# Compressed-key layers: VectorE's floors and inverses three steps ahead and behind the minima, the window keys' copies ahead of the second floor

## What is computed

```python
out = lax.map(block, (qb_all, gates, jnp.arange(n_q)))
...
s_s = jnp.einsum('btgrd,bgtnld->bgrtnl', qb, kg).astype(f32) * scale
s_s = s_s - slopes[None, :, :, None, None, None] * dist_s[:, :, None]
p_s = masked_softmax(s_s, (dist_s >= 0)[:, :, None], (-2, -1))
o_sel = jnp.einsum('bgrtnl,bgtnld->btgrd', p_s.astype(vg.dtype), vg)
...
p_w = masked_softmax(s_w, mask_w, -1)
o_win = jnp.einsum('bgrtl,blgd->btgrd', p_w.astype(vw.dtype), vw)
return gb[..., 0:1] * o_cmp + gb[..., 1:2] * o_sel + gb[..., 2:3] * o_win
...
def masked_softmax(s, mask, axis):
    s = jnp.where(mask, s, NEG_INF)
    m = jnp.max(s, axis=axis, keepdims=True)
    e = jnp.where(mask, jnp.exp(s - m), 0.0)
    return e / jnp.maximum(jnp.sum(e, axis=axis, keepdims=True), 1e-30)
```

## Time and profile before

| | before |
|---|---|
| median of 3 runs | 2573.88 us (2573.37 to 2575.04) |
| time of the profiled execution | 2574.38 us |
| its span | 2572.6 us |
| mean granted TensorE clock | 0.996 |
| busy: TensorE, VectorE, ScalarE, GpSimd | 98%, 62%, 46%, 18% |

### The profile page before, as it was taken

The page is one execution under the profiler, slowest core; times in us unless marked ns, Lnnn a source line. Parts: engine busy times, 40 slices in busy tenths (PEclk is TensorE's granted clock), DMA queues, the critical chain, the costliest instruction groups (busy, mean ns, idle before and its releaser), DMA issues.

```text
span 2572.6 us, 38307 instructions
## 1 busy us (share of the span) xinstructions
PE 2514.6 (98%) x13336; PEld 2072.8 (81%) x13336; DVE 1607.4 (62%) x2773; ACT 1184.5 (46%) x2035; POOL 467.3 (18%) x514
## 2 busy tenths in 40 slices
PE   8999999999999999999999999999999999999997
PEld 6987778888788678888878878888779778788886
DVE  7598577664353847667256677664386884766733
ACT  4467554443232845444245554443254684544431
POOL 2035321110010612111010021110010552111100
PEclk9999999999999999999999999999999999999999
DMA  4410123333233023332321123333233002233331
GB/s 160 142 34 2 42 83 98 98 98 98 87 99 99 9 66 99 98 97 90 103 85 57 42 82 99 98 98 98 79 116 122 18 2 58 87 94 97 90 106 49
DMA packets 61909, 210.91 MB, mean 82 GB/s; under 512 B 8528, under 2 KB 10320, under 8 KB 61776
## 3 DMA queue, kind: packets, MB, share of 16 engines
q1 hardware_dynamic: 61776, 209.13, 26.3%
HBM read 207.01 MB, written 2.10 MB: 81 GB/s over the span
## 4 chain that ended last, share of the span: by engine, by line
PE 91%; DVE 5%; ACT 1%; issue 1%; POOL 1%; DMA 0%; DVEq 0%; SPq 0%; POOLq 0%; ACTq 0%
PE psum L305 21%; PE psum L306 21%; PE psum L307 21%; PE psum L1310 3%; PE psum L1331 3%; PE psum L928 2%; PE psum L930 2%; PE psum L929 2%; PE psum L333 2%; PE psum L335 2%; PE psum L339 2%; PE psum L1297 1%; PE psum L1296 1%; PE psum L1093 1%; DVE h L501 1%
## 5 line engine op out<-in xcount | busy, mean ns | idle before, releaser
L305 PE MATMUL psum<-xh,w_hi 128*128 128x512 f32 x1712 | 666.6, 389 | 0.0
L306 PE MATMUL psum<-xh,w_lo 128*128 128x512 f32 x1712 | 666.1, 389 | 0.0
L307 PE MATMUL psum<-xl,w_hi 128*128 128x512 f32 x1712 | 666.1, 389 | 0.0
L267 DVE TENSOR_TENSOR w_lo<-w_raw,w_hi 128x1024 fp32r<-128x1024 f32 x226 | 284.1, 1269 | 527.5 <-ACT w_hi L261 525.7
L261 ACT ACTIVATE w_hi<-w_raw 128x1024 fp32r<-128x1024 f32 x226 | 236.2, 1057 | 590.6 <-PE psum L307 464.8
L307 PEld LDWEIGHTS psum<-xl,w_hi 128*128 128x128 f32 x1712 | 321.3, 188 | 66.8
L305 PEld LDWEIGHTS psum<-xh,w_hi 128*128 128x128 f32 x1712 | 321.4, 188 | 66.6 <-issue 0.2
L306 PEld LDWEIGHTS psum<-xh,w_lo 128*128 128x128 f32 x1712 | 321.4, 188 | 66.4
L709 DVE TENSOR_TENSOR w_lo<-w_raw,w_hi 128x1024 fp32r<-128x1024 f32 x160 | 209.3, 1308 | 253.6 <-ACT w_hi L705 253.6
L680 POOL TENSOR_TENSOR cv<-cv 128x512 f32<-128x512 f32 x88 | 133.9, 1521 | 793.7 <-ACT cv L634 773.0
L705 ACT ACTIVATE w_hi<-w_raw 128x1024 fp32r<-128x1024 f32 x160 | 168.4, 1052 | 234.8 <-PE psum L307 234.7
(11 more groups left out here) (221 smaller groups left out, 4027.1 us busy)
## 6 DMA issues: line engine op xcount, KB each, us to landing
w_raw<-w_up SPq DMA_DIRECT2D x176, 512.0 KB, 3.6
w_raw<-w_down SPq DMA_DIRECT2D x88, 512.0 KB, 3.6
w_raw<-nsa_in SPq DMA_DIRECT2D x56, 512.0 KB, 4.3
w_raw<-sb_in SPq DMA_DIRECT2D x24, 512.0 KB, 3.7
w_raw<-nsa_out SPq DMA_DIRECT2D x16, 512.0 KB, 3.6
w_raw<-swa_in SPq DMA_DIRECT2D x10, 512.0 KB, 3.8
w_raw<-sb_out SPq DMA_DIRECT2D x8, 512.0 KB, 3.6
w_raw<-swa_out SPq DMA_DIRECT2D x8, 512.0 KB, 3.6
```

Source lines behind the costliest of these rows:

```text
L267: nc.vector.tensor_tensor(w_lo[:, u % RING, :], w_raw[:, u % RING, :], w_hi[:, u % RING, :].bitcast(F32), ALU.subtract).then_inc(split_don ...
L305: nc.tensor.matmul(bank(p, o), wh[:, k, o, :], xhi(k), start=(first and k == 0), stop=False)
L306: nc.tensor.matmul(bank(p, o), wl[:, k, o, :], xhi(k), start=False, stop=False)
L307: mm = nc.tensor.matmul(bank(p, o), wh[:, k, o, :], xlo(k), start=False, stop=(last and k == 1))
```

## The change

The loop of VectorE is put into another order. In iteration t the floor and the inverse of step t + 2 become the floor and the inverse of step t + 3, side by side, and they stand behind `biased(t + 4)`. Before, the floor stood at the head of the iteration and a copy (i = 2 and 3) stood between it and the inverse. Ahead of the loop, `window_keys` comes between the first and the second floor, and `floor(2)` and `inverse(2)` go ahead of the loop. No instruction is added, removed or changed.

```diff
@@ -1468,25 +1468,24 @@
             mark = [0]
             biased(0)
             biased(1)
-            for t in range(2):
-                floor(t)
-                inverse(t)
+            floor(0)
+            inverse(0)
             window_keys()
+            floor(1)
+            inverse(1)
             biased(2)
             biased(3)
+            floor(2)
+            inverse(2)
             for t in range(STEPS):
                 it, x = t // 16, t % 16
-                i = step_of(t)[3]
-                if i == 0:
+                if step_of(t)[3] != 1:
                     copy(t)
-                if t + 2 < STEPS:
-                    floor(t + 2)
-                if i >= 2:
-                    copy(t)
-                if t + 2 < STEPS:
-                    inverse(t + 2)
                 if t + 4 < STEPS:
                     biased(t + 4)
+                if t + 3 < STEPS:
+                    floor(t + 3)
+                    inverse(t + 3)
                 if it == 0 and 1 <= x <= 8:
                     window_low(x - 1)
                 if it + 1 < G and x in (9, 10, 13, 14):
```

## The result

The changed kernel takes 2583.1 us, the median of 7 runs (2581.79 to 2583.87), where the kernel before took 2574.35 us in 7 runs. The ratio is 1.0034, with a 95% interval of 1.0024 to 1.0044. The change makes the kernel 0.34% slower. The profiled execution of it took 2583.87 us, with a span of 2582.1 us.

What follows compares the result with a forecast made beforehand. TensorE was taken to bound the kernel at its own pace. Per layer 4.7 us lost minus 1.4 regained made 3.3, 6.6 for two, on 2574.38: 2581.0, with the median 0.5 lower at 2580.5 us; range 2575.5 to 2585.5.

Steps and rivals of the forecast that it cites:

- That copies come late at three places: Floors at x = 14, 10 and 2 delay VectorE's copies; TensorE waits 0.84, 0.42, 0.27 us; chance 0.56.
- The pass that I expected at 35.5 us: A pass of 16 steps in the changed kernel takes about 35.5 us, where it took 34.03.
- I take all 1.20 us of pass 0: Pass 0, mainly step 12: floors ahead of query instructions start GpSimd's weights earlier and win back 1.20 us per layer.
- my lower bound of 0.6: Smallest gain allowed for pass 0 from floors ahead of the query instructions: 0.6 us, with 1.20 the upper bound.
- the shift past the preparation of the keys: Earlier steps of pass 0: floors moved ahead of key preparation should win the rest of step 12's 1.13 us wait.
- places that I had at 0.1 us together: x = 2 and 6 of pass 0, behind a shorter copy of keys: 0.1 us lost together, bounds 0 and 0.5.
- The port: Pass 0, floor of x = 10: GpSimd's weights of step 12 could hold it and the copy up to 1.0 us.
- The gain is at most 0.23 us: Layer start: window keys' copies without the second floor ahead gain at most 0.23 us, taken as 0.2 per layer.
- The sum: Per layer, 4.7 us lost to late copies and 1.4 us regained, net 3.3 us; 6.6 us for two layers.
- VectorE falls behind for good: Rival: late copies push later ones, pass 0's 1.2 us is not won, the port adds 1.0; 2586.1 us; chance 0.18.
- The signs of being wrong: Passes still at 34.0 us, TensorE waiting for anything but L1440, or ScalarE's exponentials moving earlier against TensorE.
- always ends after it: Shared ports of VectorE and GpSimd: a floor issued behind a GpSimd weight always ends after that weight.

Runs made afterwards that it cites:

- Loop alone: The changed kernel's loop with the start of the kernel before, and step 2's floor and inverse behind that start; 2583.32 us, ratio 1.0036 to the kernel before.
- the other instructions ahead: The changed kernel with key preparation, query instructions and finished outputs' instructions put back ahead of the floor and inverse; 2574.88 us, ratio 1.0002 to the kernel before.
- the run without the floor: The changed kernel with the floor left out of the loop and the inverse taken of the raw sums; 2575.89 us.
- the start alone: The kernel before with only the window keys' copies moved between the first and second floor, loop unchanged; 2569.92 us, ratio 0.9983.
- two ahead: The changed kernel with the floor and inverse behind the minima being those of two steps ahead, not three; 2590.08 us, ratio 1.0062 to the kernel before.
- one step ahead: The kernel before with the changed start, plus pass 0's floor and inverse of step 12 moved from step 10 to step 9; 2569.31 us, ratio 0.9982.
- deferred: The changed kernel, but behind i = 1 steps the floor and inverse come only after the next step's copy; 2574.59 us, ratio 1.0 to the kernel before.
- the first four experiments: Changed start only, changed loop only, other instructions back ahead of the floor, floors behind i = 1 steps postponed; 2569.92, 2583.32, 2574.88, 2574.59 us.

## Why the prediction was right, and where not

*That copies come late at three places* was right, in mechanism and place. I had 0.84, 0.42 and 0.27 us; they are 0.92, 0.50 and 0.23 us, and the step times there grew by 0.91, 0.43 to 0.49 and 0.20 us. TensorE does pay for them in full and catches nothing up. Loop alone, the other instructions ahead and the run without the floor each moved these stalls as the queue says. The pass that I expected at 35.5 us takes 35.65.

*"I take all 1.20 us of pass 0"* was the wrong step. Step 11 to step 12 takes 1.93 us where it took 2.54, so 0.61 us were won: GpSimd's weights start earlier by what the query instruction no longer takes. That this meets my lower bound of 0.6 is in part luck, since 2.54 was the longest of its kind. In layer 3, and in the second profile of the kernel before, the same step took 2.34 to 2.40 us, so that only 0.4 to 0.5 us were won against them. The other half, which the shift past the preparation of the keys should win, was not. VectorE prepares the keys in pass 0 and has little time to spare (before, it was busy 32.65 of 34.64 us there and 28.47 of 34.01 in pass 1), and copies came late at places that I had at 0.1 us together. By the step times, steps 4, 5, 8 and 9 lose 0.62, 0.19, 0.30 and 0.19 us, and steps 0 and 1 lose 0.39 and 0.14 us. The changed kernel, pass 0, at step 4 (timeline):

```profile
166.10 0.61 POOL L1516 CAST kh<-kts 64x512 fp32r<-64x512 f32 x1
166.14 0.59 DVE L1461 TENSOR_SCALAR rsums<-rsums 128x2 f32<-128x2 f32 x1 [0.81 <-ACT scores L1376]
...
166.77 0.17 DVE L1466 RECIPROCAL rsums<-rsums 128x2 f32<-128x2 f32 x1
...
166.96 0.42 DVE L1451 CAST kl<-kl 64x512 fp32r<-64x512 f32 x1
...
167.42 0.42 DVE L1440 COPY pt<-psum 128x256 f32<-128x256 f32 x1
...
167.90 0.42 PEld L1310 LDWEIGHTS psum<-ident,scores 128*128 128x128 f32 x4 [0.64 <-DVE pt L1440]
```

and at step 12:

```profile
183.64 3.74 POOL L1510 TENSOR_SCALAR scores<-scores,rsums,gat 128x512 f32<-128x512 f32 x4 [1.16 <-DVE rsums L1466]
...
185.71 0.42 PEld L1310 LDWEIGHTS psum<-ident,scores 128*128 128x128 f32 x4 [0.75 <-POOL scores L1510]
...
186.58 0.42 PEld L1310 LDWEIGHTS psum<-ident,scores 128*128 128x128 f32 x4 [0.45 <-DVE pt L1440]
```

*The port.* I had counted it only as a bound at one place, up to 1.0 us for the floor of x = 10. There the floor was not held: it takes 0.17 us and ends while the weights still run (last section), and the query instruction behind it takes 0.80 in place of 0.69 us. The port acts at another place: at 166.14 us a floor of two columns takes 0.59 us, as long as GpSimd's copy of keys beside it, which is 0.42 us over an undisturbed one, and the rows behind it follow closely up to TensorE's 0.64 us wait. In pass 0 of the changed kernel five of 17 floors take 0.41 to 0.59 us. The holds are hardly more than before (the 17 floors take 4.61 us together, and took 4.38), but a copy that TensorE wants stands behind them now. The run without the floor shows the sum of all that, 1.8 us in pass 0 against 0.67 us each in passes 1 and 2. How much of the 1.8 us is the hold and how much the floors' own 0.2 us each in a full queue, no run here tells apart.

*"The gain is at most 0.23 us"* at the start was wrong as well, and in the other direction: it is 1.24 us to step 0, of which 0.39 us are lost again at step 1, where ScalarE's copy is not there yet. I reasoned that TensorE's idle time began at 155.32 us and that the copies began at 155.55, so I let the copies start when TensorE's product was finished. But the copies read the window keys' product, which is older. Their only hindrance was VectorE's queue, the second floor with its 0.83 us for ScalarE, its inverse included. So they move up by all of that and the wait of 1.61 us shrinks to 0.34. The changed kernel's timeline:

```profile
155.30 0.17 DVE L1461 TENSOR_SCALAR rsums<-rsums 128x2 f32<-128x2 f32 x1
155.50 0.17 DVE L1466 RECIPROCAL rsums<-rsums 128x2 f32<-128x2 f32 x1
155.58 1.27 DVE L1013 TENSOR_TENSOR kts<-psum,rb 128x512 f32<-128x512 f32 x2
...
156.97 0.39 PE L1296 MATMUL psum<-kh,qs 128*128 128x256 f32 x1 [0.34 <-DVEq L1888]
```

*The sum.* For a layer I had +3.5 us in the steps and -0.2 at the start. It is +6.05 and -1.24, so +4.8 us. Of the 6.05 us the three expected places make 4.73 (three each of about 0.91 and 0.20, and 0.43, 0.47 and 0.49 at x = 12), where I had 4.59; the rest of pass 0 makes +1.20, where I had 0.1 - 1.2 = -1.1; the last 0.1 us lies at x = 1 of the later passes. The errors of pass 0 and of the start, 2.3 and 1.0 us, offset each other in part, which is luck, and why 2580.5 us came near 2583.1 us. Twice 4.8 is 9.6 us, and the medians differ by 8.75 us. The falls of the clock, of which the kernel before has more, can account for that, but no trace is of a median.

*The rivals.* "VectorE falls behind for good", 2586.1 us, described pass 0 better than the forecast did (half of the 1.2 us is not won, and held floors add to the loss) but not the others, which stay at the three places and at a steady 35.65 us. The forecast had the start as a gain and the loop as a loss, but with 0.4 us in all for the start it gave no reason to try the start alone.

*The signs of being wrong.* The profile after shows one of them: at step 12 of pass 0 TensorE still waits 0.75 us for GpSimd, where I had expected under 0.4 us and no wait but for L1440.

## What to carry to other kernels

Before moving a waiting instruction ahead in an in-order queue, add up what will stand behind it when it waits: a wait that costs its own engine nothing is paid by whoever needs the last of those. Before capping the gain of an earlier instruction by the idle time that one sees, find out what it really reads; if that is old, only the queue holds it and the whole wait can go. And where a change does two things, run each alone: here, by the traces, one part was worth -2.4 us and the other +11.

## What the runs showed of the hardware

**The granted clock falls for 3.4 us after a wait, but not each time.** Where TensorE has stood still for 1.58 to 1.85 us, at a layer's start or ahead of L333 (matmuls outside the changed part, which wait for ScalarE's L561), the granted clock in some executions goes to half, 1.2 GHz, 0.5 to 1.5 us after the wait's end. In the ten profiles 13 of 70 waits ahead of L333 are followed by such a fall, and 3 of 6 at a layer's start. The kernel before at layer 3's start, by windows (us, busy time with instructions of PE, PEld, DVE, ACT, POOL, then PEclk, DMA share, GB/s):

```profile
2008.00:2009.50 1.50, 0.00 (x1) 0.00 (x0) 1.44 (x4) 1.46 (x4) 1.50 (x3) 1.00 0.00 0
...
2010.50:2011.00 0.50, 0.50 (x5) 0.50 (x5) 0.50 (x5) 0.41 (x1) 0.12 (x1) 0.57 0.06 16
2011.00:2012.00 1.00, 1.00 (x6) 1.00 (x6) 0.49 (x5) 1.00 (x5) 0.00 (x0) 0.50 0.00 0
2012.00:2013.00 1.00, 1.00 (x5) 0.90 (x4) 0.49 (x1) 1.00 (x5) 0.00 (x0) 0.50 0.00 0
...
2013.80:2015.00 1.20, 1.20 (x10) 1.02 (x8) 1.08 (x5) 0.48 (x2) 1.14 (x3) 0.92 0.00 0
```

The same place in layer 0, by windows, in the first profile of the kernel before:

```profile
159.00:160.00 1.00, 1.00 (x7) 0.74 (x7) 0.93 (x4) 1.00 (x5) 0.00 (x0) 1.00 0.00 0
```

and in the second:

```profile
159.00:160.00 1.00, 1.00 (x7) 1.00 (x6) 0.61 (x7) 1.00 (x5) 0.00 (x0) 0.50 0.00 0
```

So the fall belongs neither to the layer nor to the instructions. At a layer's start it costs some 1.4 us: pass 0 takes 36.06 to 36.11 us with a fall and 34.64 us without. Most of it lies in the step from 0 to 1, which takes 3.26 us in the second profile's layer 0 in place of 1.82. Between the layers it costs about 0.6 us, and this can be counted. The stretch from step 63 of layer 0 to step 0 of layer 3 holds no changed code but layer 3's start; with 1.24 us added back for kernels that have the new start:

| profile | falls in it, at us | stretch, us |
|---|---|---|
| loop alone; two ahead; no floor; one step ahead | none | 1718.15; 1718.17; 1718.12; 1718.14 |
| start alone | none | 1718.22 |
| before, second profile | 343 | 1718.74 |
| before, first profile | 341, 1498 | 1719.27 |
| after | 347, 712 | 1719.29 |
| others ahead of the floor | 343, 1500 | 1719.33 |
| deferred | 343, 708, 1500 | 1719.93 |

This is one thing that keeps the medians from adding up. Another lies ahead of the steps: the first matmul of `scores(0)` stands at 150.45 us in the earliest of the ten profiles and at 151.94 in the latest, with no fall of the clock before it and no changed instruction. Of the 9.5 us between the spans of the first two profiles 1.3 us are of this kind, and no run here tells what makes them. The 27 runs of the kernel before beside the first four experiments lie from 2572.57 us at a mean clock of 0.998 to 2576.76 us at 0.994. The start alone was at 0.998 in 10 of 11 runs, so it gains 2.4 us by its own work, and the rest goes with fewer falls: the long wait at each layer's start is gone, and at the other places none is in its profile. What decides whether a wait is followed by a fall is not shown here. A gain of 2 us, as in start alone, should be read from the trace and not from the medians alone.

**A tiny VectorE instruction can last as long as GpSimd's.** Besides the floors above, the query instruction takes 0.69 us alone and 1.10 us at 181.65 beside the weights (step 12 one step ahead), and a pair of weights of 512 columns 1.52 us alone (two steps ahead) and 2.00 to 2.01 us beside a query. The Trainium skill, SBUF — State Buffer, section Who interferes with whom, says of VectorE's instructions in a two-port mode, for which it names `tensor_scalar`, that of the two engines the one that issues first keeps the shared ports and the other fully blocks. The held floors agree with that. Thirteen floors in seven profiles do not: they start 0.07 to 0.10 us after a weight and take at most 0.21 us, while the weight runs on. In the changed kernel the second weight of step 12 runs from 184.89 to 185.66 us, and this floor ends 0.5 us before it:

```profile
184.98 0.17 DVE L1461 TENSOR_SCALAR rsums<-rsums 128x2 f32<-128x2 f32 x1
```

So the prediction's "always ends after it" goes too far. Why these are spared is not shown, and the floor at 166.14, which was held, started only 0.04 us after a copy of keys. The same section says that VectorE's instructions with at most one SBUF input and outside the two-port modes don't contend; the inverses would fit it, which took at most 0.17 us in every run, beside GpSimd or not. The weight that starts 0.07 us behind the query at 180.12 takes 1.26 us in place of 0.77, so it loses 0.5 us of the 0.6 us in which the two run together.
